# Early routing of the cold blocks' first head, and the delta inverse in packed blocks of 64

## The reference, cut to what matters

```python
qr = (xt @ w_q).reshape(t, PEER_HEADS, 2, PEER_DK // 2)
sc = jnp.einsum('thpd,hpnd->thpn', qr, subkeys)
s1, i1 = lax.top_k(sc[:, :, 0], PEER_TOPK)
s2, i2 = lax.top_k(sc[:, :, 1], PEER_TOPK)
cand = (s1[..., :, None] + s2[..., None, :]).reshape(t, PEER_HEADS, PEER_TOPK * PEER_TOPK)
best, flat = lax.top_k(cand, PEER_TOPK)
experts = (e1 * PEER_NKEYS + e2)
hid = jnp.einsum('cd,ced->ce', xc, jnp.take(u, ec, axis=0))
out = jnp.einsum('ce,ced->cd', gc * gelu(hid), jnp.take(v, ec, axis=0))
```

```python
lmat = jnp.where(strict, jnp.einsum('bhnik,bhnjk->bhnij', kb, k) * decay, 0.0)
tmat = triangular_solve(lmat + eye, eye, lower=True, unit_diagonal=True)
```

## Time and profile before

| | |
|---|---|
| median of 3 runs | 2396.09 us (2393.96 to 2404.05) |
| profiled execution, its own time | 2393.64 us |
| its span | 2391.8 us |
| TensorE busy | 1953.3 us (82%) |
| VectorE busy | 1644.3 us (69%) |
| ScalarE busy | 807.2 us (34%) |
| moved by DMA | 746.74 MB, 312 GB/s over the span |
| mean granted TensorE clock | 0.904 |

### The profile page before, as it was taken

How to read it: one execution, slowest core, us unless ns; L and a number is a source line. 1 busy time by engine, 2 the same in 40 slices (tenths; PEclk the granted TensorE clock), 3 DMA queues, 4 the chain that set the end, 5 groups by cost and what they waited for, 6 DMA issues and landing times. The chain is left out here.

```text
span 2391.8 us, 31710 instructions
## 1 busy us (share of the span) xinstructions
PE 1953.3 (82%) x11848; PEld 1286.6 (54%) x11848; DVE 1644.3 (69%) x3769; ACT 807.2 (34%) x1826; POOL 665.9 (28%) x657
## 2 busy tenths in 40 slices
PE   3999996788785689879959987885878774999798
PEld 3887886664341146546526554641444332868684
DVE  5668876487968577655486888757798544379763
ACT  3112222134342342553343366325323224243322
POOL 2222110044354333433433335334434340000000
PEclk9998998898897789999969999996898996999899
DMA  8998763189999999999989989999999993322200
GB/s 329 360 367 308 261 250 115 36 351 419 371 407 421 421 413 418 419 419 411 402 334 391 390 317 414 418 403 369 358 419 416 419 419 137 111 71 82 86 10 27
DMA packets 124682, 746.74 MB, mean 312 GB/s; under 512 B 13536, under 2 KB 16480, under 8 KB 56304
## 3 DMA queue, kind: packets, MB, share of 16 engines
q0 software_dynamic: 93792, 610.66, 63.4%
q1 hardware_dynamic: 30736, 134.05, 14.6%
HBM read 741.25 MB, written 3.41 MB: 311 GB/s over the span
## 5 line engine op out<-in xcount | busy, mean ns | idle before, releaser
L1809 POOL DMA_INDIRECT got<-in_peer_uv,idx x512 | 590.8, 1154 | 915.8 <-PE ps L1773 800.2
L1906 DVE CUSTOM_DVE_ANT_0 got<-got,xk 128x1024 f32<-128x1024 f32 x512 | 619.7, 1223 | 328.3 <-DMA got<-in_peer_uv,idx 325.7
L1773 PE MATMUL ps<-got,diag 64*64 64x512 f32 x3936 | 583.1, 686 | 210.2 <-ACT diag L1866 156.0
L1861 ACT ACTIVATE gelu<-eye,hid 128x64 f32<-128x64 f32 x492 | 170.6, 347 | 780.8 <-DVE hid L1906 779.4
L1773 PEld LDWEIGHTS ps<-got,diag 64*64 64x64 f32 x3936 | 122.2, 144 | 468.6 <-ACT diag L1866 302.1
L1342 PE MATMUL ps<-xT,ring 128*128 128x256 f32 x928 | 232.3, 398 | 0.0
L1342 PEld LDWEIGHTS ps<-xT,ring 128*128 128x128 f32 x928 | 174.7, 197 | 74.4 <-issue 53.1
L1866 ACT ACTIVATE diag<-gelu,gate 128x64 f32<-128x64 f32 x492 | 171.0, 348 | 45.8 <-ACT gelu L1861 0.8
L1028 PE MATMUL ps<-xT,ring 128*128 128x256 f32 x768 | 184.1, 388 | 2.6 <-ACT xT L1143 2.6
L1028 PEld LDWEIGHTS ps<-xT,ring 128*128 128x128 f32 x768 | 140.2, 190 | 75.2 <-issue 50.3
L192 POOL DMA_DIRECT2D vring<-in_vslabs x136 | 72.2, 532 | 276.1 <-DVE in_b_psums L304 137.8
(11 more groups left out here) (591 smaller groups left out, 2539.9 us busy)
## 6 DMA issues: line engine op xcount, KB each, us to landing
ring<-in_small SPq DMA_DIRECT2D x158, 512.0 KB, 7.9
vring<-in_vslabs POOLq DMA_DIRECT2D x136, 512.0 KB, 6.3
ring<-in_slabs SPq DMA_DIRECT2D x18, 2048.0 KB, 10.4
got<-in_peer_uv,idx POOLq DMA_INDIRECT x512, 12.8
h<-in_x SPq DMA_DIRECT2D x2, 2048.0 KB, 11.4
w_out<-in_slabs SPq DMA_DIRECT2D x2, 2048.0 KB, 10.1
out<-h SPq DMA_DIRECT2D x4, 512.0 KB, 2.6
bias_rows<-brow POOLq DMA_DIRECT2D x1, 1280.0 KB, 4.8
```

What stands on the lines that cost most here:

```text
L1773: mm = nc.tensor.matmul(ps[to:to + HALF, i, :], diag[own, d % NDIAG, :], got[own, n % GRING, 1, 512 * g:512 * g + 512], start=(k == 0), st ...
L1809: nc.gpsimd.indirect_dma_start(out=got[:, n % GRING].rearrange("p a d -> p (a d)"), out_offset=None, in_=table, in_offset=bass.IndirectOff ...
L1861: nc.scalar.activation(gelu_of[:, n % 2, :], eye2[:], ACT.Gelu, scale=hid[:, w % 2, k:k + 1]).then_inc(gelu_done, 1)
L1906: nc.vector.tensor_tensor_reduce(row_in, row_in, xk[:, w % 2, :], 1.0, 0.0, ALU.mult, ALU.add, hid[:, w % 2, k:k + 1]).then_inc(dotted, 1)
```

## The change

The first part is in `peers`. The first head's two score products of a cold block (4 and 6) are made by themselves (`cold_scores`), one slot after the second ask job is evicted, and taken out of PSUM by themselves (`take_cold`); its `halves`, `pairs`, `name` and `shift` follow in the next slots. The other six products are made where all eight were made before, and taken in the piece that also does the softmax of head 0. `SIDE_END` is 57 in place of 53, so both mixings are paced over 111 slots, and the turns and scores stand four slots later.

The second part is in `delta_tiles`. The two diagonal blocks of 64 of each head's matrix are kept packed, the first in partitions 0 to 63 and the second in 64 to 127, with 64 columns a head: `lb`, `cs`, `xnb`, `xtb`, `ycb` are 128 x 256. Levels 0 to 5 work on both blocks at once (`in_blocks`: eight products of 64x64x64, on the corner of the array of the own half), and the last level joins them by products across the halves (`across`) and writes the whole `xt`. There are six masks of 64 columns, and the identity stands as a seventh.

```diff
             BEHIND = 2
-            SIDE_END = 53
+            SIDE_END = 57
...
+            cold_at = {}
+            for w in COLD[1:]:
+                p = (w - NT) // 2
+                asked = min(s for s, some in side_plan(p)["evac_at"].items() if any(job[1:] == ("ask", 1) for job in some))
+                cold_at[1 + min(n for n, (side, until) in side_steps.items() if side == p and until > asked)] = w
+
...
-                    return [SIDE_END + 4 + i for i in range(FIRST)]
+                    first = min(n for n, x in cold_at.items() if x == w + 1) % SLOTS + 1
+                    pairs_at = max(first + 2, FOLD % SLOTS + 2 if w == NT + 1 else 0)
+                    return [first, first + 1] + [pairs_at + i for i in range(FIRST - 3)] + [SIDE_END + 5]
                 return [8 + 3 * i for i in range(LATER)] if w < NW - 1 else []
...
+
+                def take_cold():
+
+                    step.eng.wait_ge(cold_scored, COLD.index(w))
+                    ve.tensor_copy(sc[:, 0:2, :], ps[:, 3, 0:2 * P].rearrange("p (g n) -> p g n", g=2)).then_inc(cold_taken, 1)
+                    step.eng.wait_ge(cold_taken, COLD.index(w))
+
+                def take_rest():
+
+                    step.eng.wait_ge(scored, w + 1)
+                    ve.tensor_copy(sc[:, 2:6, :], ps[:, 2, :].rearrange("p (g n) -> p g n", g=4))
+                    ve.tensor_copy(sc[:, 6:8, :], ps[:, 3, 0:2 * P].rearrange("p (g n) -> p g n", g=2)).then_inc(taken, 1)
+                    step.eng.wait_ge(taken, w + 1)
...
-                pieces.append(take if w else begin)
+                pieces.append(begin if w == 0 else take_cold if w in COLD else take)
...
                     if w == 0:
                         pieces[FIRST - 1] = lambda: (take_first([1, 2, 3]), softmax(0, 1))
+                    else:
+                        pieces[FIRST - 1] = lambda: (take_rest(), softmax(0, 1))
...
                     def scores(w):
                         pe.wait_ge(made_out, made_by(w) if w else NQ)
-                        if w in COLD and w:
+                        early = 2 if w in COLD else 0
+                        if early:
                             pe.wait_ge(sides[(w - NT) // 2]["ask_out"], H)
+                            pe.wait_ge(cold_taken, COLD.index(w))
                         pe.wait_ge(keys_loaded, 16 * (w // NT + 1))
-                        for g in range(2 * PH):
-                            mm = nc.tensor.matmul(ps[:, 2 + g // 4, P * (g % 4):P * (g % 4) + P], qr[:, g, P * (w % 2):P * (w % 2) + P],
+                        for g in range(early, 2 * PH):
+                            c = P * ((g - early) % 4)
+                            mm = nc.tensor.matmul(ps[:, 2 + (g - early) // 4, c:c + P], qr[:, g, P * (w % 2):P * (w % 2) + P],
                                                   keys[:, g, :], start=True, stop=True)
                         mm.then_inc(scored, 1)
+
+                    def cold_scores(w):
+
+                        pe.wait_ge(made_out, made_by(w - 1))
+                        pe.wait_ge(sides[(w - NT) // 2]["ask_out"], 2)
+                        pe.wait_ge(keys_loaded, 16 * (w // NT + 1))
+                        for g in range(2):
+                            mm = nc.tensor.matmul(ps[:, 3, P * g:P * g + P], qr[:, g, P * (w % 2):P * (w % 2) + P], keys[:, g, :],
+                                                  start=True, stop=True)
+                        mm.then_inc(cold_scored, 1)
...
+                                if w in COLD:
+                                    pe.wait_ge(cold_taken, COLD.index(w))
...
+                        if n in cold_at:
+                            cold_scores(cold_at[n])
...
+    HALVES = [slice(HALF * i, HALF * i + HALF) for i in range(2)]
+
+    def blocks(x, i=0):
+
+        return by_head(x.rearrange("p h x -> p (h x)")[:, HA * HALF * i:HA * HALF * (i + 1)])
...
-               "low": tl["decay"], "cs": [tl["ct"], tl["kbT"]]}
+               "low": tl["decay"], "cs": [blocks(tl["ct"], 0), blocks(tl["ct"], 1)], "lb": blocks(tl["kbT"]),
+               "xnb": blocks(tl["xn"], 0), "xtb": blocks(tl["xn"], 1), "ycb": blocks(tl["knT"])}
...
-        lev = lambda n: levels[:, n, :].unsqueeze(1).broadcast_to([P, HA, P])
-        eye = ident.unsqueeze(1).broadcast_to([P, HA, P])
+        lev = lambda n: levels[:, n, :].unsqueeze(1).broadcast_to([P, HA, HALF])
+        eye = lev(L - 1)
+        packed = lambda t, b: blocks(bank(t, b))
+        first_half, second = HALVES
...
+            def in_blocks(b, lhs, rhs):
+                for a in range(HA):
+                    for own in HALVES:
+                        mm = nc.tensor.matmul(packed(t, b)[own, a, :], lhs[own, a, :], rhs[own, a, :], start=True, stop=True)
+                return mm
+
+            def across(b, to, frm, lhs, rhs):
+                for a in range(HA):
+                    mm = nc.tensor.matmul(packed(t, b)[to, a, :], lhs[frm, a, :], rhs[frm, a, :], start=True, stop=True)
                 return mm
...
             elif k == EYE:
-                pe.wait_ge(sg["c"], L * u + 1)
-                turn(2, tl["ct"]).then_inc(sg["y"], 1)
+                pe.wait_ge(sg["c"], (L - 1) * u + 1)
+                for a in range(HA):
+                    for own in HALVES:
+                        mm = nc.tensor.matmul(packed(t, 2)[own, a, :], tl["cs"][0][own, a, :], ident[own, own], start=True, stop=True)
+                mm.then_inc(sg["y"], 1)
...
-                pe.wait_ge(sg["c"], L * u + n + 1)
                 pe.wait_ge(sg["x"], (L - 1) * u + n)
-                heads(1, tl["cs"][n % 2], tl["xn"]).then_inc(sg["y"], 1)
+                if n < L - 1:
+                    pe.wait_ge(sg["c"], (L - 1) * u + n + 1)
+                    in_blocks(1, tl["cs"][n % 2], tl["xnb"]).then_inc(sg["y"], 1)
+                else:
+                    across(1, second, first_half, tl["lt"][:, :, second], tl["xnb"]).then_inc(sg["y"], 1)
...
                 if n < L - 1:
-                    heads(2, tl["xt"], tl["yc"]).then_inc(sg["za"], 1)
-                heads(0, tl["yc"], tl["xt"]).then_inc(sg["zb"], 1)
+                    in_blocks(2, tl["xtb"], tl["ycb"]).then_inc(sg["za"], 1)
+                    in_blocks(0, tl["ycb"], tl["xtb"]).then_inc(sg["zb"], 1)
+                else:
+                    across(0, first_half, second, tl["ycb"], tl["xtb"]).then_inc(sg["zb"], 1)
...
-                nc.scalar.activation(tl["yc"], bank(t, 1), ACT.Copy).then_inc(sg["yc"], 1)
+                made = slice(0, P) if n < L - 1 else second
+                nc.scalar.activation(tl["ycb"][made], packed(t, 1)[made], ACT.Copy).then_inc(sg["yc"], 1)
...
-                step(ve.tensor_tensor(tl["lt"], bank(t, 1), tl["decay"], ALU.mult))
-                ve.tensor_tensor(tl["ct"], tl["lt"], lev(0), ALU.mult).then_inc(sg["c"], 1)
-                dve.wait_ge(sg["c"], L * u + 1)
-                step(ve.tensor_tensor(tl["xt"], eye, tl["ct"], ALU.subtract))
+                for own in HALVES:
+                    step(ve.tensor_tensor(tl["lb"][own], bank(t, 1)[own, :, own], tl["decay"][own, :, own], ALU.mult),
+                         but=0 if own == second else 1)
+                ve.tensor_tensor(tl["lt"][first_half, :, second], bank(t, 1)[first_half, :, second],
+                                 tl["decay"][first_half, :, second], ALU.mult)
+                ve.tensor_tensor(tl["cs"][0], tl["lb"], lev(0), ALU.mult).then_inc(sg["c"], 1)
+                dve.wait_ge(sg["c"], (L - 1) * u + 1)
+                step(ve.tensor_tensor(tl["xtb"], eye, tl["cs"][0], ALU.subtract))
             elif k == EYE:
                 dve.wait_ge(sg["y"], L * u + 1)
-                ve.tensor_tensor(tl["xn"], eye, bank(t, 2), ALU.subtract).then_inc(sg["x"], 1)
-                ve.tensor_tensor(tl["cs"][1], tl["lt"], lev(1), ALU.mult).then_inc(sg["c"], 1)
+                ve.tensor_tensor(tl["xnb"], eye, packed(t, 2), ALU.subtract).then_inc(sg["x"], 1)
+                ve.tensor_tensor(tl["cs"][1], tl["lb"], lev(1), ALU.mult).then_inc(sg["c"], 1)
                 dve.wait_ge(sg["la"], 2 * u + 2)
...
-                if n < L - 1:
-                    ve.tensor_tensor(tl["cs"][(n + 1) % 2], tl["lt"], lev(n + 1), ALU.mult).then_inc(sg["c"], 1)
+                if n < L - 2:
+                    ve.tensor_tensor(tl["cs"][(n + 1) % 2], tl["lb"], lev(n + 1), ALU.mult).then_inc(sg["c"], 1)
+                elif n == L - 1:
+                    ve.memset(tl["xt"][second, :, first_half], 0.0)
+                    dve.wait_ge(sg["xs"], (L - 1) * u + n - 1)
+                    for own in HALVES:
+                        ve.tensor_copy(tl["xt"][own, :, own], tl["xtb"][own])
...
                 if n < L - 1:
                     dve.wait_ge(sg["za"], (L - 2) * u + n)
                     dve.wait_ge(sg["x"], (L - 1) * u + n)
-                    ve.tensor_tensor(tl["xn"], tl["xn"], bank(t, 2), ALU.subtract).then_inc(sg["x"], 1)
```

(16 more changed lines are left out.)

7 lines of the change are left out of this document (4 added, 3 removed).

## The result

The changed kernel takes 2359.15 us (median of 4 runs, 2353.03 to 2364.41) beside 2399.64 us for the kernel before (4 runs): a ratio of 0.9834, 95% interval 0.9806 to 0.9862. That is 40.5 us less, clear of the noise, though under 2%. In two later comparisons the same kernel had 0.9873 (0.9858 to 0.9887), 30.5 us less, and 0.9856 (0.9836 to 0.9876), 33.0 us less.

What follows compares the result with a forecast made beforehand. Idle transfers were to be won in the expert stage; TensorE bounds the second block, except VectorE around tile 1. 2393.6 - 17.5 (routing) - 17.5 (inverse) = 2358.6, plus 2.4 for the median: 2361 us, range 2348 to 2387.

Steps and rivals of the forecast that it cites:

- rival (a): Delta inverse: the two corners take turns at the PSUM bank, costing 3 us a tile at TensorE's bound; 2388 us; chance 0.18.
- Rival (b): Blocks 4 and 6: VectorE's remaining routing pieces set the pace, idle moves behind the boundary; gain 3 us, total 2373; chance 0.13.
- the low end: Lower end of the forecast range for the whole kernel, given as 2348 us, with routing gaining 23 and the inverse 24.
- with 9.7 us less on it before, about half goes: Block 4, 1244 to 1260 us: relieving VectorE at the boundary removes about half of 6.1 us of idle transfers.
- I take a fourth: Block 6, 1665 to 1695 us, VectorE 28.2 of 30 us busy: a fourth of 6.9 us of idle transfers goes.
- forecast 2: Both mixings paced over 111 slots in place of 107 by `SIDE_END` 57: gain 2 us, between 0 and 4.
- 5.6 for tile 0: Second block, tile 0, bound by TensorE: its inverse falls from 15.7 to 10.1 us, 5.6 us less.
- 4.3 for tile 1: Second block, tile 1, bound by VectorE: narrower level instructions take 4.3 us less.
- 9 for tiles 2 and 3: Second block, tiles 2 and 3: gain between VectorE's 8.6 and TensorE's 11.2 us, taken as 9.
- 0.16 us for going in and out: Delta inverse on TensorE: each visit of corner products costs 0.16 us beyond 0.445 us for a group with corners abreast.
- 0.28 + 0.73 = 1.01: One level's groups on TensorE: y from 0.89 to 0.61 us, z pair from two of 0.89 to 0.89 + 0.16.
- Rival (c): Second block's bound stretches: TensorE's clock falls as less of its time is filled; 2479 us if all; chance 0.04.

Runs made afterwards that it cites:

- e7: Changed kernel with every `in_blocks` group issued twice over, same products into the same places: 2382.95 us, ratio 0.9944.
- e1: Kernel before with only the cold blocks' early first head and `SIDE_END` 57, delta inverse still in products of 128: 2382.16 us, ratio 0.9936.
- e11: Changed kernel with routing of heads 1 to 3 in blocks 4 and 6 moved off the blocks' opening: 2369.35 us, ratio 0.9881.
- e4: Kernel before with only the cold blocks' early first head; `SIDE_END` left at 53, old inverse: 2385.34 us, ratio 0.9945.
- e9: Changed kernel with side programs let in one step a slot for six slots, then at most three steps in two slots: 2368.9 us, ratio 0.989.
- e10: Changed kernel run again unchanged, beside the version with the smooth start of the side programs: 2363.41 us, ratio 0.9856.

## Why the prediction was right, point by point

**Right in mechanism.** The two waits for `idx` go and the two boundaries fill; no wait of TensorE arises at slots 47 and 49, and VectorE's level instructions take 0.42 us. The corners run abreast: rival (a) is out. The Trainium skill ("TensorEngine Tiling (Array Packing)", Restrictions and Gotchas) says that different row tiles can't access the same PSUM bank at once. For this layout, two row tiles that write different partitions of one bank, the trace doesn't agree: sixteen instructions cost 0.47 us (e7) where turns would take 0.9. Rival (b) is out too, since the idle didn't move; it stood there before.

**The total agrees in part by luck.** The forecast was 17.5 + 17.5 = 35 us. The two parts gave 13.2 + 15.5 = 28.7 by the profiles, and the same kernel measured 40.5, 30.5 and 33.0 us below the kernel before in three comparisons. That the first median, 2359.15, lies 2 us from 2361 says less than the stages do. Two of the prediction's sums slip without weight: rival (b) by its own terms is 2375.5 and not 2373, and the low end is 2349.

**Part one, forecast 17.5 us, measured 13.2** (by e1's median 14.4, 12 to 18). What failed is a mechanism, the step "with 9.7 us less on it before, about half goes". Won were the boundaries' own 5.8 + 4.8 = 10.6 us, and the places behind them are as large as before. The first hangs on the chain of the mixing's opening, ScalarE's squares and roots, and not on VectorE (e11, and the wait of 6.86 us in the kernel before). For the second, "I take a fourth" named the right engine in part, it seems, since e11 won 2.2 us there by moving pieces off it; but relief ahead of the boundary didn't reach it. The rest of part one, some 3 us, fits `SIDE_END` (forecast 2, measured 0 to 7.4). The place where the prediction looked for that gain, 1360 to 1430, is no smaller than before (11.2 us, then 11.6), so where it falls stays open.

**Part two, forecast 17.5 us, measured 15.5.** By stretches: last dot to the first mask product of tile 0 +0.8 us, to tile 1's -2.4, to tile 2's -4.7, to tile 3's -0.7, to the end -8.5. Forecast were 5.6 for tile 0, 4.3 for tile 1, 9 for tiles 2 and 3 (9.1 measured). Tile 1's 4.7 is not all the inverse's: e1 and e4, with the old inverse, have 1.6 and 1.7 of it. From its first mask product to its last write tile 1 took 50.9 us before and takes 47.1, at a granted clock of 1.00 in both: 3.8 us. Tile 0 is off most, for two reasons.

The first is a term that was mis-sized: "0.16 us for going in and out". Inside a group it is right (0.61 - 0.47 = 0.14), but the neighbours pay too. One level of tile 0 on TensorE, after the change:

```profile
2036.37 0.68 PE L2053 MATMUL ps<-rows 64*64 64x64 f32 x16
2036.98 2.00 PE L1342 MATMUL ps<-xT,ring 128*128 128x256 f32 x8
2038.91 1.34 PE L2587 MATMUL ps<-by_bucket,rwide 32*128 32x320 f32 x4
2040.18 1.15 PE L2053 MATMUL ps<-rows 64*64 64x64 f32 x32
2041.26 1.99 PE L1342 MATMUL ps<-xT,ring 128*128 128x256 f32 x8
2043.18 0.68 PE L2053 MATMUL ps<-rows 64*64 64x64 f32 x16
```

The same level in the kernel before:

```profile
2051.43 1.05 PE L1993 MATMUL ps<-rows 128*128 128x128 f32 x8
2052.32 1.89 PE L1342 MATMUL ps<-xT,ring 128*128 128x256 f32 x8
2054.14 1.34 PE L2506 MATMUL ps<-by_bucket,rwide 32*128 32x320 f32 x4
2055.41 1.16 PE L1993 MATMUL ps<-rows,dl_x 128*128 128x128 f32 x8
2056.40 1.06 PE L1993 MATMUL ps<-dl_x,rows 128*128 128x128 f32 x8
2057.30 1.89 PE L1342 MATMUL ps<-xT,ring 128*128 128x256 f32 x8
2059.03 1.05 PE L1993 MATMUL ps<-rows 128*128 128x128 f32 x8
```

From start to start:

| part of the level | before, us | after, us |
|---|---|---|
| y group | 0.89 | 0.61 |
| eight projection instructions behind it | 1.82 | 1.93 |
| four instructions of 32*128 | 1.27 | 1.27 |
| pair of z groups | 1.89 | 1.08 |
| eight projection instructions behind it | 1.73 | 1.92 |
| level | 7.60 | 6.81 |

The groups themselves save 1.09 us, near the forecast's 0.28 + 0.73 = 1.01 (the z pair before already had an edge in front of it, behind the instructions of 32*128). The projections give 0.30 of it back: between full-width products they take 1.73 us, with one change of the tile size at an end 1.82, with two 1.92 to 1.93. So each edge between instructions of different tile size costs about 0.10 us, outside the group's own row. A level saves 0.8 us. A tile has thirteen visits of corner products; with two new edges each they are at most 2.6 us, an estimate from these rows, and the forecast of 5.6 would then be 3.0 or a little more.

The second is the clock. In the 20 us from 40 us behind the last dot, where tile 0 begins, the granted clock was 0.74 before and is 0.67 after: TensorE, fully busy there, is at its lower level (1.2 GHz) from about 36 us behind the last dot until 50 us before the change and until 53 us after it. (0.74 - 0.67) x 20 = 1.4 us at full speed; with them tile 0 would have given 3.8. Rival (c) had named the clock, but for the bound stretches, which kept 1.00, and by less work on TensorE; that this is what delays the rise is not shown.

## What to carry to other kernels

When transfers are idle at several places in a row, price each by what its own queue waits for: relief ahead of a place doesn't reach it when another chain stands there, and that chain can be read in the profile of before. Small products in corners of the array paid here even within one bank, with neighbouring instructions in alternate corners; price a visit with its neighbours (here up to 0.14 + 2 x 0.10 = 0.34 us over 0.47 of work), not by the group's own row. A disputed engine can be judged by padding its operations, which takes one kernel and gives the answer tile by tile; read the granted clock of each tile beside it, since it differed in the same tiles.

## What the runs showed of the hardware

The clock at the start of a busy stretch was worth more than some edits. e9 and e10 have the same code behind the last dot, and 40 to 60 us behind it their windows read:

```profile
2025.20:2045.20 20.00, 20.00 (x168) 16.94 (x166) 5.74 (x15) 2.30 (x6) 0.00 (x0) 0.85 0.15 53
```

```profile
2025.40:2045.40 20.00, 20.00 (x148) 16.96 (x148) 5.74 (x15) 1.91 (x5) 0.00 (x0) 0.66 0.15 53
```

The first is e9's, the second e10's: TensorE 20.00 of 20 us busy in both, at 0.85 and at 0.66 of full clock, with 168 and 148 instructions done. 0.19 x 20 = 3.8 us, and the second block took 379.9 against 383.9 us. TensorE was busy throughout in both: e9's clock rose at 2027.8, fell again at 2031.2 and stayed full from 2034.6 on, while TensorE in the profile after the change stood at the lower level for 17 us, fully busy, from 2013 to 2030. About 2 of e1's 3.0 us with the old inverse are of this kind (0.83 against 0.74 before; its tile 0 took 97.2 against 99.2 us). In the same window the nine other executions with blocks of 64 had 0.65 to 0.68, e1 and e4, both with the early head and the old inverse, 0.83. The values repeat so closely that plain chance is unlikely; what decides when the clock rises there stays open.

The order of the corners counts: alternating, a y group of sixteen is 0.61 us ahead of its successor, one corner after the other 0.90, for the same products.
